# Turning and multiplying the first chunk of a stage token tile by token tile, at five stage borders

## The reference

```python
for l in range(2):                                   # two blocks of the first kind
    h = rms_norm(x, attn_pre_g[l]); proj = h @ w_in[l]            # stage in0, in1
    ... differential and forgetting attention ...
    x = x + rms_norm(mixed @ w_out[l], attn_post_g[l])            # stage out0, out1
    h = rms_norm(x, ffn_pre_g[l])
    y = (silu(h @ w_gate[l]) * (h @ w_up[l])) @ w_down[l]         # stages ffn0/down0, ffn1/down1
    x = x + rms_norm(y, ffn_post_g[l])
xn = rms_norm(x, norm1_g); proj = xn @ w_in_2                     # stage in2
... stick-breaking attention, HGRN2 mixer, branch2 ...
h = x + mixed @ w_out_2                                           # stage out2
hn = rms_norm(h, norm2_g)
out = h + (silu(hn @ w_gate) * (hn @ w_up)) @ w_down              # stages ffn2, down2
```

## Time and profile before

| what | value |
|---|---|
| time, median of 3 runs | 2253.09 us (2251.55 to 2256.26) |
| time of the profiled execution | 2254.23 us |
| its span, first to last instruction | 2252.4 us |
| PE busy | 95% of the span |
| PEld busy | 78% |
| DVE, ACT, POOL busy | 34%, 33%, 38% |
| mean granted PE clock | 0.983 of 2.4 GHz |

### The profile page before, as it was taken

How to read it: one execution, slowest core, us unless ns; L and a number is a source line. 1 busy time by engine, 2 the same in 40 slices (tenths; PEclk the granted TensorE clock), 3 DMA queues, 4 the chain that set the end, 5 groups by cost and what they waited for, 6 DMA issues and landing times.

```text
span 2252.4 us, 27470 instructions
## 1 busy us (share of the span) xinstructions
PE 2149.5 (95%) x10268; PEld 1760.5 (78%) x10268; DVE 768.0 (34%) x1445; ACT 742.9 (33%) x1231; POOL 846.3 (38%) x390
## 2 busy tenths in 40 slices
PE   7999999999999999999999999999788899999999
PEld 5886778888887877778888877877677677888887
DVE  5327442121013137341212023677576332221200
ACT  4236442222223136442222233544432334222221
POOL 3430134444434420234444434433344334444443
PEclk9999999999999999999999999999999999999999
DMA  6320023332333320023332322211111223333232
GB/s 190 103 84 1 11 78 109 99 96 94 101 87 94 93 75 1 29 85 98 98 93 93 98 70 75 66 57 48 47 47 38 64 76 112 94 101 95 89 103 70
DMA packets 138736, 178.21 MB, mean 79 GB/s; under 512 B 19857, under 2 KB 87697, under 8 KB 138641
## 3 DMA queue, kind: packets, MB, share of 16 engines
q1 hardware_dynamic: 137024, 175.25, 25.8%
q10 hardware_dynamic: 1616, 1.64, 0.2%
HBM read 174.76 MB, written 2.10 MB: 79 GB/s over the span
## 4 chain that ended last, share of the span: by engine, by line
PE 85%; DVE 7%; issue 5%; ACT 2%; POOL 1%; DMA 0%; POOLq 0%; ACTq 0%; SPq 0%; DVEq 0%
PE PS L1340 24%; PE PS L1342 24%; PE PS L1341 24%; PE PS L1547 3%; PE PS L1559 2%; DVE R L1252 1%; PE PS L1714 1%; POOL w_lo L505 1%; PE PS L1535 1%; PE PS L1346 1%; PE PS L1486 1%; PE PS L1621 1%; PE PS L1650 1%; DVE R L1247 1%; DVE X L1106 0%
## 5 line engine op out<-in xcount | busy, mean ns | idle before, releaser
L505 POOL TENSOR_TENSOR w_lo<-R,w_hi 128x1024 fp32r<-128x1024 f32 (+1 forms) x268 | 629.9, 2352 | 908.4 <-ACT w_hi L580 908.3
L580 ACT ACTIVATE w_hi<-R 128x1024 fp32r<-128x1024 f32 (+1 forms) x268 | 278.3, 1041 | 949.0 <-PE PS L1342 935.8
L1340 PE MATMUL PS<-xt_hi,w_hi 128*128 128x512 f32 x1120 | 446.1, 398 | 3.4 <-DVE xt_lo L924 3.4
L1342 PE MATMUL PS<-xt_hi,w_lo 128*128 128x512 f32 x1120 | 438.3, 391 | 0.0
L1341 PE MATMUL PS<-xt_lo,w_hi 128*128 128x512 f32 x1120 | 438.1, 391 | 0.0
L1340 PE MATMUL PS<-w_hi,xt_hi 128*128 128x512 f32 x928 | 382.1, 412 | 12.2 <-DVE xt_lo L924 9.7
L1342 PE MATMUL PS<-w_hi,xt_lo 128*128 128x512 f32 x928 | 365.7, 394 | 0.0
L1341 PE MATMUL PS<-w_lo,xt_hi 128*128 128x512 f32 x928 | 365.2, 394 | 0.0
L1340 PEld LDWEIGHTS PS<-xt_hi,w_hi 128*128 128x128 f32 x1120 | 211.8, 189 | 47.7 <-issue 5.3
L1342 PEld LDWEIGHTS PS<-xt_hi,w_lo 128*128 128x128 f32 x1120 | 211.6, 189 | 44.5
L1341 PEld LDWEIGHTS PS<-xt_lo,w_hi 128*128 128x128 f32 x1120 | 211.9, 189 | 43.7 <-issue 1.0
(11 more groups left out here) (231 smaller groups left out, 2228.2 us busy)
## 6 DMA issues: line engine op xcount, KB each, us to landing
R<-in_w_in SPq DMA_DIRECT2D x48, 512.0 KB, 3.7
R<-in_w_gate SPq DMA_DIRECT2D x88, 256.0 KB, 2.8
R<-in_w_up SPq DMA_DIRECT2D x88, 256.0 KB, 3.0
raw<-in_w_in SPq DMA_DIRECT2D x44, 512.0 KB, 3.6
R<-in_w_down SPq DMA_DIRECT2D x40, 512.0 KB, 3.8
R<-in_w_ffn_gate SPq DMA_DIRECT2D x44, 256.0 KB, 2.8
R<-in_w_ffn_up SPq DMA_DIRECT2D x44, 256.0 KB, 3.1
R<-in_w_ffn_down SPq DMA_DIRECT2D x20, 512.0 KB, 3.8
```

Of the source, the lines that this page charges most:

```text
L505: nc.gpsimd.tensor_tensor(w_lo[:, r, 0:subs, :], raw_of(stage)[:, r, 0:subs, :], w_hi[:, r, 0:subs, :].bitcast(F32), ALU.subtract).then_in ...
L580: nc.scalar.activation(w_hi[:, r, 0:subs, :], raw_of(stage)[:, r, 0:subs, :], ACT.Copy).then_inc(hi_ready, 1)
L1340: mm(out_, a_hi, b_hi, start=start, stop=False)
L1342: return mm(out_, a_lo, b_hi, start=False, stop=stop)
```

## The change

At the borders into ffn0, in1, ffn1, in2 and ffn2 the whole first chunk is done per token tile. XN is multiplied with the norm's gain on DVE (a row vector `pre_g`, loaded by ACT's queue into a place of its own, instead of columns in `gcol` that SP loaded at the start). `turn_tile` turns the eight k-blocks of one tile into two banks, `tile_hi` and `tile_lo` round them in two halves, and `chunk_by_tile` multiplies that tile with all four slots, turning the next tile in the middle. The turn of tile 0 stands before the last slot of the last tile of the stage before. `TAIL` becomes 2, ACT rounds slots 2 and 3 of the new stage inside `norm_follows`, and a slot of the new stage's first lap is given free (`w_used`) only in tile 3. The bank sets of the out, ffn and down stages are exchanged. In an ffn stage a product of `chunk_by_tile` moves 128 tokens in place of 512.

```diff
-        TAIL = 1
+        TAIL = 2
+        BY_TILE = ("ffn0", "in1", "ffn1", "in2", "ffn2")
+        def tile_bank(stage, t, half):
+            return turn_bank(stage) + (2 if t == 2 else 0) + half
...
@@ sync: loads at the start
-                (gcol[:, 3, :], attn_pre_g[1].rearrange("(k p) -> p k", p=P)),
-                (gcol[:, 6, :], norm1_g_2[0].rearrange("(k p) -> p k", p=P)),
-                (gcol[:, 9, :], norm2_g_2[0].rearrange("(k p) -> p k", p=P)),
...
-                    (gcol[:, 3 * l + 2, :], ffn_pre_g[l].rearrange("(k p) -> p k", p=P)),
...
@@ scalar
+            def tile_hi(stage, t):
+                for half in range(2):
+                    act.wait_ge(ts_mm, KD * TS_OF[stage] + 2 * t + half + 1)
+                    nc.scalar.activation(xt_hi[:, 4 * half:4 * half + 4, t * P:(t + 1) * P],
+                                         PS[:, tile_bank(stage, t, half), :].rearrange("p (k n) -> p k n", n=P),
+                                         ACT.Copy).then_inc(ts_hi, 1)
+            def norm_follows(n, next_stage, before):
+                before(0)
+                before(1)
+                norm_tile(n, 0)
+                before(2)
+                norm_tile(n, 1)
+                hi_first(next_stage, [2])
+                tile_hi(next_stage, 0)
+                before(3)
+                hi_first(next_stage, [3])
+                norm_tile(n, 2)
+                tile_hi(next_stage, 1)
+                norm_tile(n, 3)
+                tile_hi(next_stage, 2)
+                tile_hi(next_stage, 3)
+            def load_pre_g(gain):
+                act.dma_start(pre_g, gain.partition_broadcast(P)).then_inc(pre_in, 16)
...
@@ vector
-                V.tensor_scalar(XN[:, t, :], X[:, t, :], small[:, 5, t:t + 1], None, ALU.mult).then_inc(xn_ready, 1)
+                    dve.wait_ge(pre_in, 16 * n)
+                    V.scalar_tensor_tensor(XN[:, t, :], X[:, t, :], small[:, 5, t:t + 1], pre_g, ALU.mult,
+                                           ALU.mult).then_inc(xn_ready, 1)
+            def tile_lo(stage, t):
+                for half in range(2):
+                    ks, tok = slice(4 * half, 4 * half + 4), slice(t * P, (t + 1) * P)
+                    dve.wait_ge(ts_hi, KD * TS_OF[stage] + 2 * t + half + 1)
+                    V.tensor_tensor(xt_lo[:, ks, tok], PS[:, tile_bank(stage, t, half), :].rearrange("p (k n) -> p k n", n=P),
+                                    xt_hi[:, ks, tok].bitcast(F32), ALU.subtract).then_inc(ts_lo, 1)
+            def norm_follows(n, next_stage, before):
+                before(0)
+                before(1)
+                norm_tile(n, 0)
+                before(2)
+                norm_tile(n, 1)
+                tile_lo(next_stage, 0)
+                before(3)
+                norm_tile(n, 2)
+                tile_lo(next_stage, 1)
+                norm_tile(n, 3)
+                tile_lo(next_stage, 2)
+                tile_lo(next_stage, 3)
...
@@ tensor
+            def turn_tile(stage, t):
+                pe.wait_ge(xn_ready, T * TS_OF[stage] + t + 1)
+                if t in (1, 3):
+                    pe.wait_ge(ts_lo, KD * TS_OF[stage] + 2 * (t // 2) + 2)
+                for half in range(2):
+                    for k in range(4):
+                        last = nc.tensor.transpose(PS[:, tile_bank(stage, t, half), k * P:(k + 1) * P],
+                                                   XN[:, t, (4 * half + k) * P:(4 * half + k + 1) * P], ident[:, :])
+                    last.then_inc(ts_mm, 1)
+            def chunk_by_tile(stage, s):
+                for t in range(T):
+                    tok = slice(t * P, (t + 1) * P)
+                    for r in range(R):
+                        if t == 0:
+                            pe.wait_ge(lo_ready, 4 * LAP0[stage] + r + 1)
+                        if r % 2 == 0:
+                            pe.wait_ge(ts_lo, KD * TS_OF[stage] + 2 * t + r // 2 + 1)
+                        for sub in range(2):
+                            k = 2 * r + sub
+                            if is_ffn(stage):
+                                for j in range(4):
+                                    cols = slice(j * P, (j + 1) * P)
+                                    last = three(PS[:, 4 * s + j, tok], w_hi[:, r, sub, cols], w_lo[:, r, sub, cols],
+                                                 xt_hi[:, k, tok], xt_lo[:, k, tok], k == 0, k == KD - 1)
+                            else:
+                                last = three(PS[:, 4 * s + t, :], xt_hi[:, k, tok], xt_lo[:, k, tok], w_hi[:, r, sub, :],
+                                             w_lo[:, r, sub, :], k == 0, k == KD - 1)
+                        if t == T - 1:
+                            last.then_inc(w_used, 1)
+                        if r == 1 and t < T - 1:
+                            turn_tile(stage, t + 1)
...
@@ token_chunk, last tiles
+                        if t == T - 1 and r == R - 1:
+                            tiled()
...
@@ swiglu
+                    if isinstance(c, int) and c == 0:
+                        chunk_by_tile(stage, s)
+                        return
```

More of the change, by code:

```diff
@@ L104 @@
 FFN_SEEN = {"ffn0": 0, "ffn1": 11, "ffn2": 22}
-SETS = {"in": (3, 3), "out": (1, 1), "ffn": (0, 0), "down": (1, 1), "in2": (1, 1), "branch": (2, 2), "out2": (1, 0)}
+SETS = {"in": (3, 3), "out": (1, 1), "ffn": (0, 0), "down": (1, 1), "in2": (1, 1), "branch": (2, 2), "out2": (0, 1)}
 SET0 = {}
@@ L620, in post_tile @@
                     act.wait_ge(evac[first], SET0[stage][first] + 1)
-                nc.scalar.activation(junk[:, t, :], PS[:, 4 * (1 - first) + t, :], ACT.Square,
+                nc.scalar.activation(junk[:, t], PS[:, 4 * (1 - first) + t, :].rearrange("p (k n) -> p k n", n=P), ACT.Square,
                                      accum_out=ssq[:, 1, t:t + 1]).then_inc(half_sq, 1)
@@ L722, in product_with_post @@
                     hi_lap(stage, LAP0[stage] + lap, lap % laps)
+                    if is_down(stage) and lap == 1:
+                        act.wait_ge(h_mul, 2 * (FFN_SEEN[f"ffn{stage[-1]}"] + 11))
+                        load_pre_g({"down0": attn_pre_g[1], "down1": norm1_g_2[0]}[stage])
                 act.wait_ge(yg_done, n_post + 1)
                 for t in range(T):
-                    last = nc.scalar.activation(junk[:, t, :], PS[:, 4 * first + t, :], ACT.Square,
+                    last = nc.scalar.activation(junk[:, t], PS[:, 4 * first + t, :].rearrange("p (k n) -> p k n", n=P), ACT.Square,
                                                 accum_out=ssq[:, 0, t:t + 1])
@@ L873, in _ @@
             hi_first("ffn2", range(TAIL))
-            norm_follows(5, lambda t: None)
-            transposed_hi("ffn2", TAIL)
+            norm_follows(5, "ffn2", lambda t: None)
             swiglu("ffn2", "down2")
@@ L1115, in product_with_post @@
                 dve.wait_ge(base_ready, n_post + 1)
[L1116 removed]
+                norm_follows(n_post + 1, next_stage, tile)
             def swiglu(stage):
@@ L1143, in _ @@
                 transposed_lo(f"out{l}")
-                product_with_post(f"out{l}", 2 * l, YG_out)
-                transposed_lo(f"ffn{l}")
+                product_with_post(f"out{l}", 2 * l, YG_out, f"ffn{l}")
                 swiglu(f"ffn{l}")
-                product_with_post(f"down{l}", 2 * l + 1, YG_down)
-                transposed_lo(f"in{l + 1}")
+                product_with_post(f"down{l}", 2 * l + 1, YG_down, f"in{l + 1}")
             for c in range(2):
@@ L1430, in project @@
                     set_free(stage, c, c)
-                    token_chunk(stage, LAP0[stage] + c, c, 1, c == 0)
+                    if c == 0 and stage in BY_TILE:
+                        chunk_by_tile(stage, 0)
+                    else:
+                        token_chunk(stage, LAP0[stage] + c, c, 1, c == 0)
                 with pe.Fori(1, n // 2) as i:
@@ L1459, in chunk @@
                             k = 2 * r + sub
-                            if first:
-                                pe.wait_ge(ts_lo, KD * TS_OF[stage] + k + 1)
                             for j in range(4):
@@ L1569, in _ @@
                 transposed_start(f"out{l}")
-                two_chunks(f"out{l}")
-                transposed_start(f"ffn{l}")
+                two_chunks(f"out{l}", f"ffn{l}")
                 swiglu(f"ffn{l}")
-                two_chunks(f"down{l}")
-                transposed_start(f"in{l + 1}")
+                two_chunks(f"down{l}", f"in{l + 1}")
             for c in range(2):
                 set_free("in2", c, c)
-                token_chunk("in2", LAP0["in2"] + c, c, 1, c == 0)
+                if c == 0:
+                    chunk_by_tile("in2", 0)
+                else:
+                    token_chunk("in2", LAP0["in2"] + c, c, 1, False)
             def in2_products(c, r):
```

131 lines of the change are left out of this document (62 added, 69 removed).

## The result

The changed kernel takes 2348.3 us (median of 4 runs, 2347.28 to 2354.44) against 2253.26 us (4 runs, 2251.55 to 2256.26) on the same chip: a ratio of 1.0427, interval 1.0415 to 1.044. It is slower, as forecast, but by 95 us instead of 61: the time lies 20 us above the range of 2286 to 2328. The profiled execution took 2347.56 us.

The account below looks back on a forecast made before the run. PE, busy 95% of the span, was taken as the bound. Terms of +61.4 - 0.2 + 2.1 - 0.5 + 5 - 3.6 - 3 = +61.2 us gave 2254.2 + 61.2 - 1.1 = 2314.3 us, range 2286 to 2328.

Parts of the forecast that it names:

- The narrow products: In the first chunks of ffn0, ffn1 and ffn2, 384 load-product pairs at 0.110 us replace 96 wide products: +61.4 us.
- The step that failed: At the ffn borders, the half clock adds nothing to the narrow chunk if loads set the pace; in in1 it costs 2.3.
- the term for ffn0 and ffn1: Narrow first chunks there cost 20.5 us more each; with the border waits, +20.3 in ffn0 and +20.0 in ffn1.
- the prediction's two signs of being wrong: Narrow products starting less than 0.08 us apart, or a border stall above 12 us, would show the prediction wrong.
- POOL holds DVE: At the borders into ffn0, in1 and ffn1, POOL's rounding delays DVE twice, about 2.3 us each; PE stands still 9.3 us.
- POOL harmless: Rival: POOL doesn't hold DVE up, so ffn0, in1 and ffn1 lose 4.7 us instead of 9.3: 2292 us, chance 0.28.
- in1, in2: Border terms: in1 +2.1 us from the wait plus clock loss; in2 +5 us from later weight slots, 3.1 in its new chunk.
- The start: At the kernel's start, five loads leaving SP's list bring the second lap's weights 2.5 us sooner: -3 us with clock loss.
- worse: Rival: later tiles of in1 and in2 stall too, or narrow products stay at 0.12 us: over 2328 us, chance 0.06.

Follow-up runs that it names:

- m1: Streams of equal products alone, nothing of the reference computed: 384 products of 128 columns took 42.7 us right after wide ones, 81.5 us after a 9.00 us wait.
- e1: The changed kernel with 30 dummy products of 512 columns filling PE's wait before the first chunks of ffn0 and ffn1: 2319.54 us, ratio 1.0284.
- e4: The changed kernel with ACT rounding slots 2 and 3 together after tile 0 is turned, so POOL's two `w_lo` start later: 2322.55 us, ratio 1.0309.
- e7: The kernel before the change with dummy products filling PE's waits at the borders into ffn0, in1, ffn1 and in2: 2244.74 us, ratio 0.9962.
- e5: The changed kernel with the five gain loads put back into SP's start list, their data unused: 2355.25 us in one run.
- e10: The kernel before the change with only the five gain loads moved from SP's start list to ACT's queue: 2250.93 us, ratio 0.9985.
- e6: e4 with 12 dummy products of 512 columns in PE's wait before the first chunks of ffn0 and ffn1: 2303.24 us, ratio 1.0232.
- e8: The changed kernel with ffn first chunks by tile pairs, tile 1 rounded earlier, POOL's steps later and dummy products around tile 1's turn: 2262.9 us, ratio 1.0042.
- e9: The kernel before the change with e7's filling, altered in in2, and e10's moved gain loads: 2240.04 us, ratio 0.9936.
- m2: Streams alone, reference not computed: 192 narrow products after three wait lengths, then 96s with turns between; 96 took 20.72 us before turns, 11.13 behind them.

## Why the prediction was right in direction and wrong in size

- **The narrow products: right at 2.4 GHz.** Taken were 0.110 us per pair; ffn2 has 0.11 and its border grew by 16.7 against 16.9, and m1 gave 0.111. The Trainium skill (TensorE: Matmul & The Clock Gate, Back-to-back issue gap) gives about 81 ns for 128 columns; no stream of 128 columns here came below 0.11.
- **The step that failed:** "The half clock costs nothing in the ffn chunk, if the load and not the columns sets the pace there." The condition held (the load does set the pace, and 64 columns are no faster than 128), but the conclusion didn't follow: the load itself takes twice as long at 1.2 GHz, 0.213 us. And the low clock didn't last for 10 products, as in the kernel before, but for 35 us, since narrow products don't bring it back as wide ones do (m1). That the low clock is the cause is shown by e1, which changes only what PE does in the wait: 16.6 us a chunk, 33 in two, which is the miss. In the sum the term for ffn0 and ffn1 should have been 20.5 + 16.6 each. Neither of the prediction's two signs of being wrong appeared (products under 0.08 us apart, a stall over 12 us): it had none for this case.
- **POOL holds DVE: right.** 3.33 and 2.29 us in the profile after, and e4 takes the hold out of the chain: the wait falls from 7.33 to 3.14 (predicted 7.7 and 3.1). The rival "POOL harmless" is out for after. The hold is worth 4 us at each of three borders, 12 in all. The rival's sum (2292) had also taken in1's clock loss as nothing, without saying so; in e4 in1 was low for 3.4 us behind its shorter wait.
- **in1, in2: near enough.** +1.6 for +2.1; +7.2 for +5, of which 5.3 in chunk 1, where the prediction had 3.1. The wait itself was near that (3.4); the rest is again the low clock behind a wait, which the prediction left out here too.
- **The start: right in kind.** -5.8 against -3 in after, but the 200th product moves by some us between kernels that have the same start: 62.45 to 65.4 with the loads out of SP's list; 65.2 in e7, 68.2 in before and 69.4 in e5 with them in. The wait at 43 us was 2.40 in before, 3.87 in e5 and absent in e7. So part of the -5.8 is chance, and e10 gives the loads alone -3.4.
- **The rival "worse"** was right in its sign for the wrong reason: no later tile stalled in after (in e6 and e8 in1's second tile did, by 2 us), and it was not 0.12 us a pair, but 0.213 at the low level and 0.111 at the high one. The low clock as a lasting state had no place among the rivals, though the earlier trace rows and the clock of 0.85 in the earlier trace rows showed that it falls there. What was missing was the question of what brings it back.
- **Open:** why a return comes behind the second set of eight turns in most chunks and behind the first in one (10.2 against 34.1 us in e4's two), and why the same short waits lowered the clock in e9's ffn2 and not in three other runs.

## What to carry to other kernels

Splitting a product's moving side below 256 columns saves nothing, for each piece pays a full load: 0.103 us for 64 columns, 0.11 for 128, 0.12 for 256, 0.227 for 512. Where a clock has fallen in a wait before a change's new instructions, ask not only what it costs now but whether the new stream would let it return, and price the whole stretch at the low level as a rival of its own. Filling PE's waits with products that nobody reads was worth more here (0.4%, and 0.6% with the moved loads) than rearranging the border, and work put early on POOL must not lie beside the DVE chain that PE waits for.

## What the hardware showed that was not expected

- A stream of loads and products of 128 columns ran at 1.2 GHz for as long as it lasted after a wait (384 products, 81.5 us), with PE and PEld busy all the time; one of 256 columns was back at 2.4 GHz after 5.9 us (27 products), one of 512 after 5.2 us (12 products). Turns among narrow products did bring it back (m2).
- At 1.2 GHz a load takes 0.213 us instead of 0.111: it follows the granted clock as the columns do.
- Waits of 1.44 us left the clock up; 2.70 and 3.96 us brought it down (m2). In e4 3.14 us (2.75 idle) brought it down as well. These are single observations and give no limit: e9's ffn2 lost the clock over four waits of at most 1.33 us each.
